# A SwiGLU FFN in two phases: gate/up tiles first, then the down projection with the contraction outermost, in three passes

## What is computed

```python
hf = rmsnorm(x, norm2[l])
x = x + (jax.nn.silu(hf @ w_gate[l]) * (hf @ w_up[l])) @ w_down[l]
y = rmsnorm(x, final_norm)
```

## Time and profile before

| | |
|---|---|
| median of 3 runs | 1613.39 us (1612.88 to 1613.64) |
| the profiled execution: span from the first to the last instruction | 1610.6 us |
| mean granted TensorE clock | 0.980 of full speed |
| PE busy | 1533.3 us (95%), 9003 matmuls |
| DVE busy | 716.2 us (44%) |
| ACT busy | 351.4 us (22%) |
| DMA moved | 105.12 MB, 65 GB/s over the span |

### The profile page before, as it was taken

How to read it: one execution, slowest core, us unless ns; L and a number is a source line. 1 busy time by engine, 2 the same in 40 slices (tenths; PEclk the granted TensorE clock), 3 DMA queues, 4 the chain that set the end, 5 groups by cost and what they waited for, 6 DMA issues and landing times.

```text
span 1610.6 us, 23009 instructions
## 1 busy us (share of the span) xinstructions
PE 1533.3 (95%) x9003; PEld 1398.8 (87%) x9003; DVE 716.2 (44%) x1132; ACT 351.4 (22%) x569; POOL 132.0 (8%) x200
## 2 busy tenths in 40 slices
PE   5999999998999999998899999999999999999997
PEld 3799899997888888886598999989898989989896
DVE  5356544534566666565333333342424333332415
ACT  5354533231111111111120211112020211111012
POOL 1000000001222222211000000000000000000001
PEclk7999999997999999999899999999999999999999
DMA  5012122162122211122170201111010102010002
GB/s 195 14 43 85 53 105 91 66 209 79 40 66 65 65 59 40 64 72 72 63 277 27 75 25 57 32 46 52 26 52 26 52 26 78 26 52 26 0 0 111
DMA packets 52561, 105.12 MB, mean 65 GB/s; under 512 B 4784, under 2 KB 30320, under 8 KB 52528
## 3 DMA queue, kind: packets, MB, share of 16 engines
q1 hardware_dynamic: 52528, 104.67, 18.8%
HBM read 82.66 MB, written 22.00 MB: 65 GB/s over the span
## 4 chain that ended last, share of the span: by engine, by line
PE 45%; issue 2%; ACT 1%; DVE 1%; DMA 1%; POOL 0%; DVEq 0%; ACTq 0%; POOLq 0%
PE bank L86 15%; PE bank L88 15%; PE bank L87 15%; ACT gu_hi L1592 1%; DMA out_y<-y_out 1%; DVE acc L1678 0%; DVE y_out L1642 0%; DVE hf L1654 0%; ACT y_out L1628 0%; POOL fstat L1693 0%; DVEq L1677 0%; ACTq L75 0%; POOL fstat L1691 0%; POOLq L1510 0%; DVE gu_lo L1635 0%
## 5 line engine op out<-in xcount | busy, mean ns | idle before, releaser
L86 PE MATMUL bank<-ht_hi,w_hi 128*128 128x364 f32 (+1 forms) x576 | 190.4, 330 | 0.0
L88 PE MATMUL bank<-ht_hi,w_lo 128*128 128x364 f32 (+1 forms) x576 | 189.4, 329 | 0.0
L87 PE MATMUL bank<-ht_lo,w_hi 128*128 128x364 f32 (+1 forms) x576 | 189.4, 329 | 0.0
L1654 DVE TENSOR_TENSOR hf<-sg,bank 128x364 f32<-128x364 f32 (+1 forms) x66 | 35.1, 532 | 342.9 <-PE bank L88 340.8
L86 PE MATMUL bank<-ht_hi,gu_first_hi 128*128 128x364 f32 (+1 forms) x528 | 173.4, 328 | 1.4 <-PEq L842 1.4
L87 PE MATMUL bank<-ht_lo,gu_first_hi 128*128 128x364 f32 (+1 forms) x528 | 173.3, 328 | 0.0
L88 PE MATMUL bank<-ht_hi,gu_lo 128*128 128x364 f32 (+1 forms) x528 | 173.2, 328 | 0.0
L86 PE MATMUL bank<-ht_hi,gu_hi 128*128 128x364 f32 (+1 forms) x528 | 173.1, 328 | 0.0
L87 PE MATMUL bank<-ht_lo,gu_hi 128*128 128x364 f32 (+1 forms) x528 | 173.1, 328 | 0.0
L88 PE MATMUL bank<-ht_hi,gu_first_lo 128*128 128x364 f32 (+1 forms) x528 | 173.0, 328 | 0.0
L1678 DVE TENSOR_TENSOR acc<-acc,bank 128x512 f32<-128x512 f32 (+1 forms) x198 | 132.3, 685 | 90.3 <-PE bank L88 90.3
(11 more groups left out here) (267 smaller groups left out, 2458.6 us busy)
## 6 DMA issues: line engine op xcount, KB each, us to landing
w_raw<-in_w_in SPq DMA_DIRECT2D x24, 512.0 KB, 4.2
dn_raw<-in_w_down SPq DMA_DIRECT2D x22, 512.0 KB, 4.3
scratch_qkv<-cb_y SPq DMA_DIRECT2D x12, 512.0 KB, 2.7
qkv_in<-scratch_qkv SPq DMA_DIRECT2D x8, 768.0 KB, 6.3
gu_first_raw<-in_w_gate SPq DMA_DIRECT2D x11, 512.0 KB, 3.5
gu_first_raw<-in_w_up SPq DMA_DIRECT2D x11, 512.0 KB, 4.3
gu_raw<-in_w_gate SPq DMA_DIRECT2D x11, 512.0 KB, 3.5
gu_raw<-in_w_up SPq DMA_DIRECT2D x11, 512.0 KB, 4.3
```

The source lines that it names most:

```text
L86: pe.matmul(out, w_hi, x_hi, start=start, stop=False)
L87: pe.matmul(out, w_hi, x_lo, start=False, stop=False)
L88: return pe.matmul(out, w_lo, x_hi, start=False, stop=stop)
L1654: eng.tensor_tensor(hf[b][:, 0:m], sg[b][:, 0:m], psum[2 * b + 1][:, 0:m], ALU.mult).then_inc(hf_done, 1)
```

## The change

The FFN is done in two phases. In the first, all 22 gate/up tiles are worked off; each `hf` group is stored from SBUF to a DRAM buffer `h` (22 x 128 x 1088 floats). The steps that made `h_hi` and `h_lo`, the splits of down weights, the down matmuls and the sums into `acc` leave the pair loop.

In the second phase the down projection runs in three passes over the token tiles (three tiles each: 0 to 2, 3 to 5, and 8, 6, 7, where 8 is the tile of 64 sample tokens). A pass keeps its six output blocks in six PSUM banks and goes through all 22 contraction tiles (steps). In each step SP loads 128 rows of down weights (`wd_raw`, 512 KB) and the pass's columns of h (`hraw`, 192 KB; 160 KB in the third pass), ACT and DVE split both (`wd_hi`, `wd_lo`; `hx` holds the high part and behind it the low part), and PE does 6 x 3 matmuls. All these buffers exist twice. For the sample tile two matmuls do the work of three: one of them has high and low parts of 64 tokens side by side as its 128 columns, and the two halves of the result are added at the end (`hfold`). When a pass ends, DVE adds each bank once to the residual tile `x1`, and norm and store follow for its three tiles. The six banks of the next pass begin with the two that are free.

Because more semaphores are needed, those of the input block are released, and POOL clears them at the end of the mixer. Some keep their old name in the listings below: `const_in` counts the roots, `x_in0` the landed stores of `y_out0`.

```diff
+            numbers = sorted(sem.num for sem in k["done_with"])
+            for n in numbers:
+                if n - 1 not in numbers:
+                    last = next(m for m in itertools.count(n) if m + 1 not in numbers)
+                    eng.sem_clear(range(n, last + 1))
...
-    acc = B("acc", [P, MT, D])
-    h_hi = B("h_hi", [P, 2, T], F32R)
-    h_lo = B("h_lo", [P, 2, T], F32R)
-    dn_hi = B("dn_hi", [P, 2, D], F32R)
-    dn_lo = B("dn_lo", [P, 2, D], F32R)
...
+    UNITS = 3
+    hraw = [B(f"hraw{s}", [P, UNITS * P]) for s in range(2)]
+    hx = [B(f"hx{s}", [P, 2 * UNITS * P], F32R) for s in range(2)]
+    x1 = [B(f"x1_{u}", [P, D]) for u in range(UNITS)]
+    y_out = [B(f"y_out{s}", [P, D]) for s in range(2)]
+    hfold = B("hfold", [TS, D])
...
+    PASSES = 3
+    STEP = 2 * UNITS
...
+    def tiles_of_pass(p):
+
+        tiles = [(m, P if m < NC else TS, (m - UNITS * p) * P) for m in range(UNITS * p, UNITS * (p + 1))]
+        return tiles[-1:] + tiles[:-1] if tiles[-1][0] == NC else tiles
...
+    def out_bank(p, u, half):
+
+        return psum[(4 + STEP * p + 2 * u + half) % 8]
...
+            def store_h(j, s, g):
+                n = PAIR * j + NG * s + g
+                a, m = GROUPS[g]
+                eng.wait_ge(hf_done, n + 1)
+                b = (NG * s + g) % 2
+                eng.dma_start(scratch["h"][bass.ds(2 * j + s, 1)].squeeze(0)[:, a:a + m],
+                              hf[b][:, 0:m]).then_inc(h_out[b], 16)
...
+            def free_raw(p, j, s):
+
+                eng.wait_ge(dn_hi_done, splits(p, j, s, 1))
+                eng.wait_ge(dn_lo_done, splits(p, j, s, 1))
+
+            def store_y(p):
+                for u, (m, n, _) in enumerate(tiles_of_pass(p)):
+                    q = UNITS * p + u
+                    eng.wait_ge(y_done, q + 1)
+                    eng.dma_start(o["y"][m * P:m * P + n, :], y_out[q % 2][0:n, :]).then_inc(y_dma[q % 2], 16)
+                    if p + 1 < PASSES:
+                        m2, n2, _ = tiles_of_pass(p + 1)[u]
+                        eng.dma_start(x1[u][0:n2, :], scratch["x1"][m2 * P:m2 * P + n2, :]).then_inc(x1_in, 16)
+
+            for s in range(2):
+                eng.wait_ge(h_out[s], 16 * NP * NG)
+            for s in range(2):
+                load_h(0, s, s)
+            for p in range(PASSES):
+                def steps(j):
+                    for s in range(2):
+                        free_raw(p, j, s)
+                        load_wd(2 * j + 2 + s, s)
+                        load_h(p, 2 * j + 2 + s, s)
+
+                steps(0)
+                if p:
+                    store_y(p - 1)
+                with eng.Fori(1, NP - 1) as j:
+                    steps(j)
+                if p + 1 < PASSES:
+                    for s in range(2):
+                        free_raw(p, NP - 1, s)
+                        load_wd(s, s)
+                        load_h(p + 1, s, s)
...
-                        eng.wait_ge(acc_done, SUMS * j + (2 * (m - 2) + half + 1 if m >= 2 else 0))
-                        for s in range(2):
-                            mm = mm3(eng, psum[4 + 2 * (m % 2) + half][0:n, :], h_hi[:, s, toks], h_lo[:, s, toks],
-                                     dn_hi[:, s, cols], dn_lo[:, s, cols], s == 0, s == 1)
-                        mm.then_inc(dn_mm, 1)
...
+            for p in range(PASSES):
+                def steps(j):
+                    for s in range(2):
+                        begin = isinstance(j, int) and j == 0 and s == 0
+                        end = isinstance(j, int) and j == NP - 1 and s == 1
+                        eng.wait_ge(dn_hi_done, splits(p, j, s, 1))
+                        eng.wait_ge(dn_lo_done, splits(p, j, s, 1))
+                        for u, (m, n, at) in enumerate(tiles_of_pass(p)):
+                            for half in range(2):
+                                cols = slice(half * BANK, (half + 1) * BANK)
+                                out = out_bank(p, u, half)
...
+                                if begin and p:
+                                    late = 2 * u + half - (8 - STEP)
+                                    if late >= 0:
+                                        eng.wait_ge(acc_done, STEP * (p - 1) + late + 1)
+                                high, low = hx[s][:, at:at + n], hx[s][:, low_at(p, at):low_at(p, at) + n]
+                                if m < NC:
+                                    mm = mm3(eng, out[:, :], high, low, wd_hi[s][:, cols], wd_lo[s][:, cols],
+                                             begin, end)
+                                elif begin:
+                                    eng.matmul(out[:, :], hx[s][:, at:at + 2 * n], wd_hi[s][:, cols],
+                                               start=True, stop=False)
+                                    mm = eng.matmul(out[0:n, :], high, wd_lo[s][:, cols], start=False, stop=False)
+                                else:
+                                    eng.matmul(out[0:n, :], high, wd_lo[s][:, cols], start=False, stop=False)
+                                    mm = eng.matmul(out[:, :], hx[s][:, at:at + 2 * n], wd_hi[s][:, cols],
+                                                    start=False, stop=end)
+                                mm.then_inc(dn_mm, 1)
+
+                loop(eng, NP - 1, steps)
+                steps(NP - 1)
...
-                        eng.wait_ge(hf_done, n + 1)
-                        eng.activation(h_hi[:, s, a:a + m], hf[b][:, 0:m], ACT.Copy).then_inc(h_hi_done, 1)
...
+            def high_wd(p, j, s):
+
+                load = FT // 2 * p + j + 1
+                eng.wait_ge(wd_in[s], 16 * load)
+                if not (p == 0 and isinstance(j, int) and j == 0):
+                    eng.wait_ge(dn_mm, STEP * (FT * p + 2 * j + s - 1))
+                eng.activation(wd_hi[s][:, :], wd_raw[s][:, :], ACT.Copy).then_inc(dn_hi_done, 1)
...
+            for p in range(PASSES):
+                def steps(j):
+                    for s in range(2):
+                        high_wd(p, j + 1, s)
+                        high_h(p, j + 1, s)
+
+                loop(eng, NP - 1, steps)
+                for u, (m, n, _) in enumerate(tiles_of_pass(p)):
+                    if u < 2 and p + 1 < PASSES:
+                        high_wd(p + 1, 0, u)
+                        high_h(p + 1, 0, u)
...
+                    q = UNITS * p + u
+                    eng.wait_ge(acc_done, STEP * p + 2 * u + 2)
+                    if q >= 2:
+                        eng.wait_ge(y_dma[q % 2], 16 * (q // 2))
+                    eng.activation(y_out[q % 2][0:n, :], x1[u][0:n, :], ACT.Square, scale=D ** -0.5,
+                                   accum_out=fstat[0:n, q, 0:1]).then_inc(ssq, 1)
...
+                if p + 1 < PASSES:
+                    low_wd(p + 1, 0, 0)
+                    low_h(p + 1, 0, 0)
+                todo = tiles_of_pass(p)
...
-                        part = acc[0:n, m, half * BANK:(half + 1) * BANK]
-                        eng.wait_ge(dn_mm, SUMS * j + 2 * m + half + 1)
-                        eng.tensor_tensor(part, part, psum[4 + 2 * (m % 2) + half][0:n, :],
-                                          ALU.add).then_inc(acc_done, 1)
...
+                        eng.wait_ge(dn_mm, STEP * (FT * (p + 1) - 1) + 2 * u + half + 1)
+                        ins = eng.tensor_tensor(part, part, out_bank(p, u, half)[0:n, :], ALU.add)
...
+                    low_wd(p + 1, 0, 1)
+                    low_h(p + 1, 0, 1)
+                for u, (m, n, _) in enumerate(todo):
+                    norm_tile(UNITS * p + u, u, n)
```

More of the change, by code:

```diff
@@ L172, in input_block, with S @@
     qkv_in = Plan(nc, top)("qkv_in", [P, QKV, P])
-    S = nc.alloc_semaphore
+    made = []
+    def S(name):
+        made.append(nc.alloc_semaphore(name))
+        return made[-1]
     const_in, more_in, x_in = S("const_in"), S("more_in"), [S(f"x_in{s}") for s in range(2)]
@@ L1584, in _ @@
-            loop(eng, NP, pair)
+            loop(eng, NP, pair)
+            for p in range(PASSES):
+                def steps(j):
+                    for s in range(2):
+                        begin = isinstance(j, int) and j == 0 and s == 0
[6 more added lines that the diff above has]
+                                out = out_bank(p, u, half)
+                                if begin and not p and 2 * u + half == 4:
+                                    eng.wait_ge(hf_done, PAIR * NP)
+                                if begin and p:
[17 more added lines that the diff above has]
+                steps(NP - 1)
@@ L1621, in _, with high_h @@
+            def high_h(p, j, s):
+                eng.wait_ge(h_in[s], 16 * (FT // 2 * p + j + 1))
+                if not (p == 0 and isinstance(j, int) and j == 0):
+                    eng.wait_ge(dn_mm, STEP * (FT * p + 2 * j + s - 1))
+                eng.activation(hx[s][:, 0:width(p)], hraw[s][:, 0:width(p)], ACT.Copy).then_inc(dn_hi_done, 1)
```

(13 more changed lines are left out.)

174 lines of the change are left out of this document (96 added, 78 removed).

## The result

The change is slower: **1624.55 us** median (1624.04 to 1625.60, four runs) beside 1613.14 us of the kernel before (1610.96 to 1613.64, four runs) on the same chip. The ratio is 1.0077, 95% interval 1.0063 to 1.0091. The forecast was 1623.1 us, with a range of 1613 to 1640.

The account below looks back on a forecast made before the run. TensorE's instruction count was taken to bound the FFN, with every PE wait paid in full. Terms -10.0 - 9.0 + 7.6 + 2.1 + 12.6 + 4.2 + 2.2 = +9.7 us gave 1623.1 us, range 1613 to 1640.

Parts of the forecast that it names:

- 44 matmuls: Down projection: 1144 matmuls instead of 1188, at 0.227 us each, -10.0 us.
- `acc` waits in the pairs: Pair loop: sums into `acc` leave it, so ten pairs lose a PE wait of 0.9 us each, -9.0 us.
- idle at the switch: Between the phases: PE idles while the last `hf` is stored, loaded back and split, +7.6 us (6.3 to 8.5).
- steps of the passes: Inside the down passes: loads of 3.5 us and splits are ready before PE wants them, 0 us.
- ends of passes, short waits: Next pass's second step: DVE's six sums delay its split, so PE waits 0.5 and 1.3 us.
- ends of passes, long waits: Next pass's third step: splits stand behind a square waiting for a store, and behind its norm; PE waits 5.1 and 5.7 us.
- clock after the three gaps: After the switch and both long waits: PE at half clock for 4.5 us, +2.1 us each.
- tail: After the last matmul: sums, norms, square and stores take 13.1 us for 10.95, +2.2 us.
- the most likely rival, loads that set the step: Down passes: loads of 5.4 us give 1638 us, of 6.3 us about 35 us more, 1658 us; chance 0.12.
- The rival by which the clock holds through the gaps: Switch and ends of passes: no slow clock, 6.3 us go, 1616.8 us; chance 0.10.
- The rival by which the ends of passes are hidden: Ends of passes: third tile's square finds its buffer free, 12.6 + 4.2 us go, 1606.3 us; chance 0.08.
- the half clock at 779.78: Kernel before: after a long idle stretch PE worked at 1.2 GHz until about 784.3, 4.5 us, losing 2.1 us.

Follow-up runs that it names:

- experiment 3: The change, with three matmuls per half and step for the sample tokens and no folding of halves: 1632.84 us, ratio 1.0125 to the kernel before.
- experiment 7: The kernel before, with DVE's split of the next pair's second gate/up tile moved behind the pair's sums into `acc`: 1604.69 us beside 1613.11.
- experiment 2: The change, with the first two h pieces read back and split in the middle of the last gate/up pair: 1618.43 us, ratio 1.0031 to the kernel before.
- experiment 8: The change, with a second, unread 512 KB load of weights in each step that the split waits for: 1634.61 us, ratio 1.0135 to the kernel before.
- experiment 1: The change, with a third output buffer `y_out`: 1614.59 us, ratio 1.0004 to the kernel before.
- Experiment 5: The change, with a pass's first output store issued ahead of the load for the next pass's fourth step, and `x1` reloads later: 1622.01 us, ratio 1.0055.
- Experiment 10: The change with two output buffers, next pass's splits ahead of the third tile's square and between norms, two loads earlier, `x1` reloads later: 1607.06 us, ratio 0.9965.
- experiment 4: The change, with unused matmuls given to PE in the three long waits (22, 28 and 28): 1620.67 us, ratio 1.0049 to the kernel before.
- experiment 9: The change with a third output buffer, and the `x1` reloads moved behind the loads for a pass's seventh to twelfth steps: 1610.44 us, ratio 0.9987.

## Why the prediction was right, and where it was not

Term by term, in the order of its sum:

| term | predicted us | measured us | from |
|---|---|---|---|
| 44 matmuls | -10.0 | -10.0 | experiment 3, with its waits |
| `acc` waits in the pairs | -9.0 | -9.7 (-11.9 to -7.6) by time, -8.9 by the traces | experiment 7 |
| idle at the switch | +7.6 | +6.2 | trace; experiment 2 |
| steps of the passes | 0 | 0 | waits of PE; experiment 8 |
| ends of passes, short waits | +0.5, +1.3 | +0.2, +0.7 | trace |
| ends of passes, long waits | +5.1, +5.7 | +6.9, +7.1 | trace; experiments 1, 5, 10 |
| clock after the three gaps | +6.3 | +7.0 by spacing, 4.5 when avoided | trace; experiment 4 |
| tail | +2.2 | +2.0 | trace |
| sum | +9.7 | +11.1 (with 9.0 for the pairs, 7.0 for the clock) | span: +11.4 |

The waits are given from the end of one matmul to the start of the next at 0.227 us spacing, so they are some 0.15 us over the number that the trace prints beside them. About 0.3 us of the span's 11.4 stays unassigned, less than the start of phase two varies between traces (1.7 us).

**The mechanism was right**: which wait comes, on which engine, in which step, and what ends it. What the prediction called the most likely rival, loads that set the step, is refuted: no step inside a pass waits for its load, and twice the weights still do not slow two of three passes. (By the prediction's own working a load of 6.3 us would have cost 43 us and not 35; its range and its chances do not change with that.) The rival by which the clock holds through the gaps is refuted by the windows, and experiment 4 shows that PE's idling is the cause. The rival by which the ends of passes are hidden failed on what spoke against it, DVE's order: with a third buffer the square needs no store, and PE still waits 2.05 and 2.54 us (experiment 1). Experiment 10 changes the order and gets 1607.1 us. That this is near the rival's 1606.3 does not speak for the rival, since the square still waits for its store there.

**Sizes were off in both directions, and that the sum came within 1.4 us is in part luck.** The switch was 1.4 us too dear, since both transfers were taken from rows of larger ones: "2.6 us for 512 KB; 180 KB is less, but I take that row as it is" was too careful, as the store landed in 1.9 us, and the load, taken at 2.9, needed 2.3. The Trainium skill, "DMA: Bandwidth & Descriptors", section "Anatomy of one DMA", states the fit that the prediction left out of its sum for transfers issued by GpSimd, and SP issues these; the estimate by it, 4.9 us for both, was nevertheless nearer to this trace's 4.2 than the rows' 5.5. The short waits were 0.9 us too dear, the clock 0.7 us too cheap.

The long waits were 3.2 us too cheap together. The step that failed is "from a norm's end to the square behind it 2.73 us": that row is from the end of the kernel before, where nothing but these stores is moved. Here a load of 704 KB had been issued 1.15 us before the store and a reload of 512 KB 0.4 us behind it, on the same queue; the store took 4.8 us, and 4.4 at the other end. The load ahead is what counts. Experiment 5 takes it away and leaves a load behind the store: 3.0 us, and waits within 0.3 us of the forecast. Experiments 9 and 10 keep it and take the reload away: 4.6 to 4.8 us. The Trainium skill, "DMA: Bandwidth & Descriptors", section "Queues, rings and completion order", has descriptors of one issuing queue consumed in order on each DMA engine; a store behind 704 KB would then start late by what the load still has to move. These three experiments agree with it.

**What the change did not need.** Its two gains are real, 19 us together, and its losses were not in the idea of two phases but in its order: h is read back only when all of it is stored, and splits are queued behind a square that waits for a store, which itself stands behind a load. (The reloads ahead of urgent loads cost PE nothing yet in the change; they did once the store's wait was gone, in experiment 1.) With the order turned and a third output buffer for the tail, the same two phases run in 1596.7 us. But the second gain is also to be had without them (1604.7 us), so two phases by themselves bring about 8 us over the kernel before as experiment 7 arranges it, not 16.4.

## What to carry to other kernels

At the boundary of two pipelined loops, write down per engine what is queued behind each instruction that waits: at the ends of passes the wait itself (a square for its buffer) was free, and the splits behind it cost 7 us each and the clock besides. Take a transfer's time from a row with the same load ahead of it on the queue; a row without one was 2 us short twice. And put what is first needed late (the reloads) behind what is needed next.

## What the runs showed of the hardware that was not expected

The clock also fell behind short gaps, and not by their length alone. After gaps of 2.05 and 2.54 us (experiment 1, both ends) and 2.03 us (experiment 9, first end) the granted clock went to 0.50; after 2.56 us (experiment 9, second end) and 1.98 us (experiment 10) it stayed at 1.00, as it did after 1.39, 1.26 and 0.83 us. One gap shows it best, since all twelve traces have it: 1.4 us at the entry of the loop over pairs. Behind it the clock fell in four traces (experiments 4, 5, 7 and 9) and held in the other eight. In experiment 7, PE's timeline and a window behind it:

```profile
804.97 0.41 PE L86 MATMUL bank<-ht_hi,gu_first_hi 128*128 128x364 f32 x1 [1.43 <-PEq L842]
```

```profile
806.00:807.00 1.00, 1.00 (x6) 0.50 0.48 188
```

What tells these apart was not tried.

The prediction's shortest gap with a fall was 3.31 us, but the trace of the kernel before has one of 1.45 us some 30 us later, and the clock fell in the first microsecond after it:

```profile
773.90 1.38 PE L1073 MATMUL bank<-kn,mq 64*64 64x128 f32 x7 [1.45 <-DVE s_state L1376]
```

```profile
774.00:775.00 1.00, 1.00 (x7) 0.67 0.93 381
```

So the half clock at 779.78, which the prediction read as the effect of the wait of 4.29 us ahead of it, had begun before that wait. Slow stretches after the three long gaps lasted 3.4, 5.8 and 5.4 us of work and cost 1.7, 2.8 and 2.5 us; the prediction's one price of 2.1 us for each fits none of them well.

A 512 KB store of `y` landed in 2.6 us where only such stores moved, in 3.0 us ahead of a load, in 4.4 to 4.8 us behind one, and once in some 6 us in the same place. A 512 KB load behind three stores and three reloads took 8.1 us.
